# A post-norm encoder block on 8 cores: x1 kept in bf16 and transposed by DMA, a deeper ring for the squared-ReLU pieces, and a last FF2 tile by column halves

## What is computed

```python
def reference(x, w_in, sink, ...):
    proj = einsum('bsd,de->bse', x, w_in)                 # q 512 | k 128 | v 128 | u 512 | v_g 512
    attn = banded_window_attention(q, k, v, sink)         # |t - s| <= 128, 8 heads, 2 kv heads, ALiBi
    sgu = gelu(u) * (w_spatial @ layer_norm(gelu(v_g)) + b_spatial)   # by chunks of 128
    mixed = concat([rms_norm(attn), rms_norm(sgu)])
    x = layer_norm(ALPHA * x + mixed @ w_out)             # x1
    h = square(relu(x @ w_ff1))                           # 1024 -> 4096
    return layer_norm(ALPHA * x + h @ w_ff2)
```

## Time and profile before

| | |
|---|---|
| time, median of 3 runs | 2793.95 us (2792.86 to 2794.05) |
| the profiled execution: its own time | 2794.41 us |
| its span, slowest core (core 2) | 2792.8 us |
| spans of all cores | 2781.2 to 2792.8 us |
| TensorE matmul busy | 2645.5 us, 95% |
| VectorE, ACT, POOL busy | 1491.9, 1072.5, 955.4 us |
| mean granted TensorE clock | 0.980 of full speed |

### The profile page before, as it was taken

One profiled execution on the slowest core, in us unless ns is written; L12 is line 12 of the kernel. 1 busy time (PEld: TensorE's weight loads), 2 busy tenths in 40 slices (PEclk: granted clock), 3 DMA queues, 4 the chain that ended last, 5 costly groups with the idle time before them and its releaser, 6 DMA issues.

```text
span 2792.8 us, 57164 instructions; the slowest of 8 cores (2781.2 to 2792.8 us)
## 1 busy us (share of the span) xinstructions
PE 2645.5 (95%) x20844; PEld 1706.4 (61%) x20844; DVE 1491.9 (53%) x2558; ACT 1072.5 (38%) x2241; POOL 955.4 (34%) x661
## 2 busy tenths in 40 slices
PE   4689999999999999999999998899999999999996
PEld 2357777777677777777777676775444444444442
DVE  5876776767777777677767574111222221233222
ACT  4445555555555555555555452221111110111111
POOL 0333333333343333343333334222343322443332
PEclk8789999999999999999999999999999999999998
DMA  9744323423333433333333225663443434543431
GB/s 264 220 128 111 103 80 100 110 88 96 99 102 86 107 95 92 100 103 88 107 97 102 80 92 133 156 189 121 151 164 138 147 141 153 177 159 136 157 106 76
DMA packets 110134, 345.81 MB, mean 124 GB/s; under 512 B 11680, under 2 KB 11680, under 8 KB 99744
## 3 DMA queue, kind: packets, MB, share of 16 engines
q1 hardware_dynamic: 72208, 199.27, 20.6%
q10 hardware_dynamic: 17920, 100.67, 10.7%
q0 software_dynamic: 19728, 42.21, 10.0%
HBM read 250.10 MB, written 134.22 MB: 138 GB/s over the span
## 4 chain that ended last, share of the span: by engine, by line
PE 78%; ACT 6%; DVE 6%; issue 4%; DMA 4%; POOL 2%; DVEq 0%; ACTq 0%; SPq 0%; POOLq 0%
PE psum L836 27%; PE psum L804 23%; PE psum L760 8%; PE psum L659 4%; PE psum L673 4%; PE psum L675 4%; DMA hsc<-arena 2%; PE psum L729 2%; ACT L678 1%; PE psum L716 1%; DVE arena L689 1%; DMA arena<-w_gu 1%; PE psum L665 1%; PE psum L667 1%; PE psum L754 1%
## 5 line engine op out<-in xcount | busy, mean ns | idle before, releaser
L804 PE MATMUL psum<-arena 128*128 128x256 bf16 x8192 | 999.6, 274 | 15.8 <-ACT arena L648 9.8
L836 PE MATMUL psum<-arena 128*128 128x512 bf16 x4096 | 891.5, 379 | 4.5 <-POOL arena L858 2.3
L804 PEld LDWEIGHTS psum<-arena 128*128 128x128 bf16 x8192 | 773.2, 98 | 163.0 <-issue 56.1
L836 PEld LDWEIGHTS psum<-arena 128*128 128x128 bf16 x4096 | 399.5, 98 | 491.0 <-issue 16.6
L809 POOL TENSOR_TENSOR arena<-arena 128x512 bf16<-128x512 f32 x256 | 268.9, 1050 | 699.8 <-ACT arena L807 402.1
L807 ACT ACTIVATE arena<-psum 128x512 f32<-128x512 f32 x512 | 302.8, 592 | 370.7 <-PE psum L804 341.1
L774 POOL TENSOR_TENSOR arena<-arena 128x1024 f32<-128x1024 f32 x128 | 309.2, 2415 | 301.4 <-DVE arena L771 273.3
L843 DVE SCALAR_TENSOR_TENSOR arena<-psum,arena 128x512 f32<-128x512 f32 x128 | 88.3, 692 | 593.2 <-PE psum L836 521.6
L646 ACT ACTIVATE arena<-arena 128x1 f32<-128x1 f32 x320 | 93.3, 293 | 782.4 <-DVE arena L849 660.1
L856 POOL TENSOR_TENSOR arena<-arena 128x1024 f32<-128x1024 f32 x62 | 145.7, 2351 | 558.9 <-ACT arena L853 558.9
L809 DVE TENSOR_TENSOR arena<-arena 128x512 bf16<-128x512 f32 x256 | 214.7, 838 | 173.4 <-ACT arena L807 90.5
(11 more groups left out here) (82 smaller groups left out, 2182.4 us busy)
## 6 DMA issues: line engine op xcount, KB each, us to landing
hsc<-arena SPq DMA_DIRECT2D x256, 256.0 KB, 2.5
arena<-hsc ACTq DMA_DIRECT2D x64, 1024.0 KB, 5.3
arena<-x SPq DMA_DIRECT2D x64, 512.0 KB, 5.5
x1s<-arena SPq DMA_DIRECT2D x64, 512.0 KB, 3.4
arena<-x1s ACTq DMA_DIRECT2D x32, 1024.0 KB, 6.1
out<-arena SPq DMA_DIRECT2D x32, 1024.0 KB, 4.1
arena<-xt POOLq DMA_DIRECT2D x64, 256.0 KB, 5.2
arena<-w_ff SPq DMA_DIRECT2D x32, 512.0 KB, 5.5
```

Source lines behind the costliest of these rows:

```text
L804: R.pe(lambda e, fc=fc, ph=ph, z=z: [e.matmul(ph.ap[:, z * 256:(z + 1) * 256], lhsT=w1q[fc // 4].ap[:, c, (fc % 4) * 128:(fc % 4 + 1) * 12 ...
L836: R.pe(lambda e, s_=s_, q=q: [e.matmul(ps[s_][hf].ap, lhsT=hb[fc // 16].ap[:, fc % 16, s_ * 128:(s_ + 1) * 128], rhs=w2c[fc // 4].ap[:, fc ...
```

## The change

- A second copy of x1 goes to HBM in bf16 (`x1h`), by a casting DMA on POOL's queue, and `ff1_x` reads it with two DMA transposes on SP's queue straight into x1T. The loads into x1b, the transposes on TensorE and the copies on VectorE are gone.
- The pieces of h take turns in three buffers, and for the last three tiles in eight, which lie in hT1's space (`hx`). The halves of a piece are buffers of their own. The planner is told 680 instead of 512 elements for VectorE's square.
- The last FF2 tile is written by itself (`ff2_last`): each column half of a row half is evacuated, normalized by VectorE alone and written as soon as it is done, on SP's and ACT's queues.

```diff
+    x1h = nc.dram_tensor("x1h", [T, D], BF16).ap()
-    x1b = [A.buf(f"x1b{i}", BF16, [D]) for i in range(2)]
-    hst = [A.buf(f"hst{i}", BF16, [1024]) for i in range(2)]
+    NHST = 3
+    hst = [A.buf(f"hst{i}", BF16, [1024]) for i in range(NHST)]
+    hst2 = [[Buf(h_.ap[:, k * 512:(k + 1) * 512], f"hh{i}_{k}") for k in range(2)] for i, h_ in enumerate(hst)]
...
-    hT[1] = [over(f"hT1_{g}", BF16, [16, 256]) for g in range(2)]
+    for g in range(2):
+        ap = A2.alloc(BF16, [16, 256])
+        t = Buf(ap, f"hT1_{g}", extra=A.under(*A2.last))
+        hxgate_w = t.extra
+        flat = ap.rearrange("p a b -> p (a b)")
+        for k in range(4):
+            hx.append(Buf(flat[:, k * 1024:(k + 1) * 1024], f"hx{g}{k}"))
+            hx2.append([Buf(hx[-1].ap[:, z * 512:(z + 1) * 512], f"hx{g}{k}{z}") for z in range(2)])
+            t.extra = t.extra + [b_.lt for b_ in hx2[-1]]
+        hT[1].append(t)
+        hxw.extend(hxgate_w)
...
         R.dma("sp", lambda e: e.dma_start(out=x1s[m * 128:(m + 1) * 128, :], in_=yb.ap), [yb], [x1_lt[m]], f"x1t{m % 3}", 524288)
+        R.dma("pool", lambda e: e.dma_start(out=x1h[m * 128:(m + 1) * 128, :], in_=yb.ap), [yb], [x1h_lt[m]], f"x1u{m % 3}", 524288)
...
-            xbb = x1b[s_]
-            R.dma("pool", lambda e, m=m, xbb=xbb: e.dma_start(out=xbb.ap, in_=x1s[m * 128:(m + 1) * 128, :]),
-                  [x1_lt[m]], [xbb], f"x1b{s_}", 524288)
-            R.pe(lambda e, xbb=xbb: [e.transpose(psT.ap[:, c, :], xbb.ap[:, c * 128:(c + 1) * 128], ident.ap)
-                                     for c in range(8)], [xbb, ident], [psT], [128] * 8)
             dst = x1T[i % NX1][s_]
-            R.dve(lambda e, dst=dst: e.tensor_copy(out=dst.ap, in_=psT.ap), [psT], [dst, xgate[i]], 1024, 2)
+            R.dma("sp", lambda e, m=m, dst=dst: e.dma_start_transpose(out=dst.ap, in_=x1h[m * 128:(m + 1) * 128, :]),
+                  [x1h_lt[m]], [dst, xgate[i]], f"x1T{i % NX1}_{s_}", 262144)
...
+        if i == NI - NHXT:
+            R.dve(lambda e: e.memset(nmr1[0].ap, 0.0), [], [hxg, nmr1[0]] + hxw, 1)
         for g in range(8):
-            hs = hst[hn[0] % 2]
-            hkey = f"hst{hn[0] % 2}"
+            if i >= NI - NHXT:
+                j = hn[0] % len(hx)
+                hs, h2, hkey, hg = hx[j], hx2[j], f"hx{j}", [hxg]
+            else:
+                j = hn[0] % NHST
+                hs, h2, hkey, hg = hst[j], hst2[j], f"hst{j}", []
...
-                eng(lambda e, hs=hs, r_=r_, k=k: e.tensor_tensor(out=hs.ap[:, k * 512:(k + 1) * 512], in0=r_.ap, in1=r_.ap,
-                                                                 op=ALU.mult), [r_], [hs], 512)
+                eng(lambda e, hk=h2[k], r_=r_: e.tensor_tensor(out=hk.ap, in0=r_.ap, in1=r_.ap, op=ALU.mult),
+                    [r_] + hg, [h2[k]], 512 if k else 680)
...
+    def ff2_last(i):
+        hb, yo = hT[i % NHT], x1r[i % 3]
+        ps = psY[i % 2]
+        for s_ in range(2):
+            p = s_
+            yh = [Buf(yo.ap[:, s_, hf * 512:(hf + 1) * 512], f"yh{s_}{hf}", extra=[yo.lt] if s_ == 0 and hf == 0 else []) for hf in range(2)]
+            for hf in range(2):
+                for q in range(8):
+                    R.pe(lambda e, s_=s_, q=q, hf=hf: [e.matmul(ps[s_][hf].ap, lhsT=hb[fc // 16].ap[:, fc % 16, s_ * 128:(s_ + 1) * 128],
+                                                                rhs=w2c[fc // 4].ap[:, fc % 4, hf * 512:(hf + 1) * 512],
+                                                                start=(fc == 0), stop=(fc == 31)) for fc in range(q * 4, q * 4 + 4)],
+                         [hb[q // 4], w2c[q]], [ps[s_][hf]], [512] * 4)
...
+            for hf in range(2):
+                R.dve(lambda e, hf=hf, p=p, y_=yh[hf]: e.scalar_tensor_tensor(
+                    out=y_.ap, in0=y_.ap, scalar=rstdB[p].ap, in1=B2.ap[:, hf * 512:(hf + 1) * 512],
+                    op0=ALU.mult, op1=ALU.add), [yh[hf], rstdB[p], B2], [yh[hf]], 512)
+                R.dma("sp" if hf == 0 else "act", lambda e, s_=s_, hf=hf, y_=yh[hf]: e.dma_start(
+                    out=out[i * 256 + s_ * 128:i * 256 + (s_ + 1) * 128, hf * 512:(hf + 1) * 512], in_=y_.ap),
+                    [yh[hf]], [], f"outl{s_}{hf}", 262144)
```

More of the change, by code:

```diff
@@ L342, in build_nc @@
     NB = T // 128
+    NHXT = 3
     LAG0, LAG1, GROW = 2, 6, 2
@@ L387, in build_nc @@
     x1_lt = [LT(f"x1s{m}") for m in range(NB)]
+    x1h_lt = [LT(f"x1h{m}") for m in range(NB)]
     h_lt = [[LT(f"h{i}_{g}") for g in range(8)] for i in range(NI)]
@@ L469, in build_nc @@
     NX1 = 3
+    A.off = (A.off + 7) // 8 * 8
     for i in range(NX1):
@@ L475, in build_nc @@
     rl = [A.buf(f"rl{i}", F32, [512]) for i in range(2)]
-    hst = [A.buf(f"hst{i}", BF16, [1024]) for i in range(2)]
+    NHST = 3
+    hst = [A.buf(f"hst{i}", BF16, [1024]) for i in range(NHST)]
+    hst2 = [[Buf(h_.ap[:, k * 512:(k + 1) * 512], f"hh{i}_{k}") for k in range(2)] for i, h_ in enumerate(hst)]
+    A.cover([b_.lt for h2 in hst2 for b_ in h2])
     W1OFF = A.off
@@ L490, in over @@
         return Buf(ap, name, extra=A.under(*A2.last))
+    hxw = []
+    hxg = LT("hxg")
     w2c = [over(f"w2c{q}", BF16, [4, D]) for q in range(8)]
@@ L496, in build_nc @@
     hT[0] = [over(f"hT0_{g}", BF16, [16, 256]) for g in range(2)]
-    hT[1] = [over(f"hT1_{g}", BF16, [16, 256]) for g in range(2)]
+    hT[1] = []
+    hx, hx2 = [], []
+    for g in range(2):
[9 more added lines that the diff above has]
+        hxw.extend(hxgate_w)
     x1r.append(over("x1r0", F32, [2, D]))
@@ L854, in ff2 @@
                                                      bias=nmrB[p].ap, scale=rstdB[p].ap), [yo, nmrB[p], rstdB[p]], [yo], 1024)
-            aff = R.dve if i == NI - 1 else R.pool
+            aff = R.pool
             aff(lambda e, s_=s_: e.tensor_tensor(out=yo.ap[:, s_, :], in0=yo.ap[:, s_, :], in1=G2.ap, op=ALU.mult),
@@ L861, in ff2 @@
               [yo], [], f"out{i % 3}", 1048576)
+    def ff2_last(i):
+        R.tag = f"ff2{i}"
+        R.at(1000.0 + i, 1.0, 50)
+        hb, yo = hT[i % NHT], x1r[i % 3]
[4 more added lines that the diff above has]
+            for hf in range(2):
+                sl = slice(hf * 512, (hf + 1) * 512)
+                for q in range(8):
[3 more added lines that the diff above has]
+                         [hb[q // 4], w2c[q]], [ps[s_][hf]], [512] * 4)
+                R.dve(lambda e, s_=s_, hf=hf, y_=yh[hf]: e.scalar_tensor_tensor(
+                    out=y_.ap, in0=ps[s_][hf].ap, scalar=1.0 / ALPHA, in1=y_.ap, op0=ALU.mult, op1=ALU.add),
+                    [ps[s_][hf], yh[hf], yo], [yh[hf]], 512)
+                R.dve(lambda e, hf=hf, p=p, y_=yh[hf]: e.bn_stats(out=stB[p].ap[:, hf * 6:(hf + 1) * 6], in_=y_.ap), [yh[hf]], [stB[p]], 512)
+            R.dve(lambda e, p=p: e.bn_aggr(out=mvB[p].ap, in_=stB[p].ap), [stB[p]], [mvB[p]], 52)
+            rsqrt(mvB[p].ap[:, 1:2], mvB[p], epsB, 1.0, lnvB[p], rstdB[p])
+            for hf in range(2):
+                R.dve(lambda e, hf=hf, p=p, y_=yh[hf]: e.scalar_tensor_tensor(
+                    out=y_.ap, in0=y_.ap, scalar=mvB[p].ap[:, 0:1], in1=G2.ap[:, hf * 512:(hf + 1) * 512],
+                    op0=ALU.subtract, op1=ALU.mult), [yh[hf], mvB[p], G2], [yh[hf]], 512)
+            for hf in range(2):
+                R.dve(lambda e, hf=hf, p=p, y_=yh[hf]: e.scalar_tensor_tensor(
+                    out=y_.ap, in0=y_.ap, scalar=rstdB[p].ap, in1=B2.ap[:, hf * 512:(hf + 1) * 512],
[3 more added lines that the diff above has]
+                    [yh[hf]], [], f"outl{s_}{hf}", 262144)
@@ L897, in build_nc @@
             ff2_load(i + 2)
-        ff2(i)
+        if i < NI - 1:
+            ff2(i)
+        else:
+            ff2_last(i)
     R.emit(nc, es)
```

2 lines of the change are left out of this document (1 added, 1 removed).

## The result

The changed kernel takes 2877.87 us (median of six runs), the kernel before 2794.0: a ratio of 1.0289, 95% interval 1.0273 to 1.0305. It is **slower by 2.9%**, some 81 us; forecast was 2740 us, 54 us faster. The profiled execution took 2878.85 us, its span is 2877.1 us. Some executions of every kernel run with a lower clock on one die and take longer; the ratios and run times here leave them out, the medians don't.

A forecast was written before the change was run, and what follows sets the result against it. The prediction took TensorE, with 78% of the chain of waits, as the bound. Gains of 26 (transposes), 15 (stall) and 14 (end), less 1 (ring of eight), made 54 us: 2740 us, range 2722 to 2766.

The forecast's parts named there:

- 26 + 15 - 1 + 14: Whole kernel: gains from transposes, stall and end, less new waits from the ring of eight; 54 us faster in all.
- if TensorE waits for ACT at FF1 all through the middle stage: Middle stage: stated sign of being wrong, together with VectorE's squares waiting for writes of h; no size given.
- 64 x 0.45 = 28.8: Middle stage: upper bound in us for taking 64 groups of eight transposes off TensorE; 26 us was taken.
- FF1 itself isn't waited for: FF1: DMA transposes are issued two tiles ahead of use, so they cost zero, with 0 to 15 us for the range.
- The filler rival: Middle stage: TensorE's transposes stood in holes and three buffers don't hold the slow writes; 37 us gained, 2757 us, chance 0.15.
- The stall ... 15 us.: 1680 to 1820 us, FF2's weights loading beside FF1: more buffers for h gain 15 us, bounds 5 and 24.
- new waits: End of FF1: ring of eight uses hT1's space, so tile 1's load waits on ACT's queue; 1 us lost, 0 to 4.
- The end. 14 us: FF2's last tile: output by column halves and a covered wait for POOL's affine gain 14 us, bounds 8 and 14.5.
- SP, POOL and the price of a DMA transpose: DMA queues: 64 casting writes on POOL and 64 DMA transposes on SP were counted as costing zero.
- Near 5 us: SP's queue: expected time of one DMA transpose, hidden in the middle stage, where 17.7 us of hold-up is free.
- the slower transpose: FF1-only part: rival with DMA transposes of 11 to 12 us, mostly hidden, costing 13 us; 2753 us, chance 0.15.
- the bound of SP's queue: Middle stage: rival with transposes holding SP's queue beyond 17.7 us, making it slower; at 20 us 2887 us, chance 0.07.

The follow-up runs named there:

- e2: The kernel before with only the DMA transposes and the bf16 copy of x1 added: ratio 0.9967 to the kernel before, 9.2 us gained.
- e5: The kernel before with only FF2's last tile written by column halves: ratio 0.9946 to the kernel before, 15 us gained.
- e8: e1 without the ring of eight buffers (the ring of three stays): ratio 0.9905 to the kernel before, 2767 us.
- e1: The whole change with the planner's weight of VectorE's square back at 512 instead of 680: ratio 0.9949 to the kernel before, median 2777 us.
- e3: The kernel before with only the planner's weight of VectorE's square at 680 instead of 512: ratio 1.0147 to the kernel before, 2835 us.
- e13: The whole change with planner weight 560 instead of 680: ratio 1.0023 to the kernel before, 2801 us.
- e6: The whole change, weight 680 kept, with a ReLU moved ahead of the root on ScalarE's list where none stood there: ratio 1.0042 to the kernel before, 2806 us.
- e4: The whole change with the two halves of a piece of h as one buffer again: ratio 1.0286 to the kernel before.
- e9: e8 with each block's sgu matmuls one FF1 group later on TensorE's list: runs 2760 to 2764 us, ratio 0.987 to the kernel before.
- e12: The kernel before with only each block's sgu matmuls moved one FF1 group later on TensorE's list: ratio 1.0021 to the kernel before.
- e11: e8 with one load of w_ff2 instead of two behind each of FF1's last tiles: median 2764.97 us, ratio 0.9883 to the kernel before.
- e7: e1 with the loads of hT for FF2's first two tiles put later on ScalarE's queue: ratio 0.9929 to the kernel before, runs 2772 to 2776 us.
- e10: e8 with hT's first loads tied to the DMA transposes of FF1's last tile but one: median 2768.35 us, ratio 0.9894 to the kernel before.

## Why the prediction was wrong

**The ledger**, in us against the kernel before, from the ratios:

| part | forecast | measured | from |
|---|---|---|---|
| transposes off TensorE | -26 | -9 | e2 |
| end by column halves | -14 | -15 | e5 |
| third buffer and halves | with the ring, -15 | -2 | e8 less e2 and e5 |
| ring of eight | in the line above, and +1 | +12 | e1 less e8 |
| planner weight 680 | none | +95 | change less e1 |
| sum | -54 | +81 | |

Each measured number compares programs whose whole order the planner made anew, and has an interval of several us, so that -2 is not told from zero, and the parts need not add up in another kernel: the weight alone costs 41 us in the kernel before (e3) and 95 in the change.

What the time is made of can be summed from the traces. Mean of the eight cores of the profiled execution, in us: the span, all of TensorE's waits above 0.15 us, what the clock took (1 less the granted clock, over the time that TensorE was busy), and what lies behind its last matmul:

| kernel | span | waits | clock | behind |
|---|---|---|---|---|
| before | 2787.0 | 126.7 | 29.0 | 20.2 |
| e5, end alone | 2771.2 | 124.6 | 27.1 | 8.1 |
| e2, transposes alone | 2777.1 | 137.5 | 34.8 | 20.1 |
| e3, weight 680 alone | 2821.4 | 152.9 | 33.2 | 20.3 |
| e8, no ring of eight | 2759.7 | 131.7 | 34.8 | 8.4 |
| e1, weight 512 | 2769.2 | 137.1 | 37.7 | 8.8 |
| e13, weight 560 | 2798.8 | 159.2 | 46.2 | 8.8 |
| e6, ReLU ahead | 2800.4 | 175.2 | 29.4 | 8.8 |
| the change | 2866.7 | 199.5 | 72.6 | 8.8 |

From e1 to the change the span grows by 97.5 us: 62.4 in waits and 34.9 by the clock. e6 takes back 66.3: 24.3 in waits, 43.3 by the clock, the two together a little more than the whole.

**The step that failed: the new order of the instructions was put at nothing.** The sum, 26 + 15 - 1 + 14, has no term for it, although the section on the change says that the planner is told 680 instead of 512; what stood there was worth 95 us. "The other engines matter where it waits for them" was right; no step asked which instruction stands before which after the change. Its warning, "if TensorE waits for ACT at FF1 all through the middle stage", came true, but with another cause than the "squares waiting for writes of h" it gave: e3 has the wait with the old squares and ring, e4 keeps it with undivided pieces, e6 takes 69 of the 95 us away by ScalarE's list alone, and e13 lies between.

**"64 x 0.45 = 28.8", of which 26.** The price was right, what comes back wasn't. By the table, e2 has 10.7 us more of waits than the kernel before and 5.8 more by the clock; its span is 9.9 us shorter, so 26.4 us of work left TensorE. Of the 10.7 us, 6.3 lie in the first 210 us, which the prediction left alone: 4.4 of them (5.5 on the profiled core) are FF1's first matmul behind the first DMA transpose, against "FF1 itself isn't waited for". In the middle stage the waits are 34.0 us instead of 33.0: those for VectorE's normalised v grew from 6.0 to 19.3, and the others fell by nearly as much, the 8.0 us of the earlier trace rows to 3.4. But four of the new ones are 1.8 us long, and the granted clock fell to 0.72 behind three of these four. The rest, 3.4 us, lies behind 1680 us. The filler rival (22.5 - 5 for these) had the nearer number, by luck: the sum of the waits in the middle didn't grow, which was its reason. e9 shows what a better order there is worth, some 5 us, and e12 that the same move brings nothing where the transposes still stand.

**"The stall ... 15 us."** It had two errors. The slow writes didn't stay as long as they were: one of 19.1 us in e1 and 17.7 in e8 takes the place of 9 to 12, and a third buffer was to give 3.5. It isn't the ring that makes them slow, since e2, with two buffers, has one of 15.9; two loads of FF2's weights run beside the slowest, and with one of these (e11) it takes 12.9. How much is due to those loads and how much to the added writes and transposes was not separated. And the ring of eight, whose "new waits" I priced at 1 us, costs 12. Here what is shown is the sum (e8); that hT1's load on ScalarE's queue is the way in which it costs is read from the chains, and e7 and e10, which moved such loads, gave back 6 us at best. By the table the spans differ by 9.5 us, 5.4 in waits and 2.9 by the clock. The rest of it is open.

**"The end. 14 us": right**, 15 in e5. The steps are nearly as described: 12 us less behind TensorE's last matmul where 10 was forecast, and some 4 us of waits and clock; the wait for GpSimd's affine was halved, not covered.

**SP, POOL and the price of a DMA transpose: right**, but for the first one. "Near 5 us" was 3.7, with 1.23 us of the queue for each; neither the slower transpose nor the bound of SP's queue occurred. The Trainium skill's figure (VectorE: DVE Perf Modes, The three transpose paths), 1309 ns per 128x128 block, would have made it an estimated 10.5 us for eight in a row; the measured 3.7 us (8.0 at most) speaks against that use. The section after it, Rules for kernel authors, advises TensorE where a PSUM destination will do; here the way by DMA gains 9 us (e2), a third of what leaves TensorE, so the measurement goes against the advice, though not by much.

**The slower squares** (1067 ns on average, before 838) are explained by the traces. A square on VectorE beside which no GpSimd tensor instruction runs takes 0.69 us in both: 218 of the 256 before, 131 after. The others take 1.72 us on average before and 1.47 after. They meet 38 times before, 67 in e1 and 125 in the change, so that the new order has its part; e6 shows that this isn't what cost the time.

What stays open: how the 12 us of the ring of eight divide.

## What to carry to other kernels

Where a program orders the instructions from costs, every number in a diff that feeds those costs is a change of its own: print the new order at the engines the bound one waits for, and look at what stands between a producer and the instruction that frees a bank. Undo that number alone first. Work taken from the bound engine counts only so far as no other wait opens in its place; look at the start of the program and at single long waits, not only at their sum in the middle. Each extra buffer taken from another stage's space moves a load there, and a load on a compute engine's queue holds all behind it.
